# Experts and last sums of a two-block transformer in the block of the routing, without the two joins of all engines

## Reference, cut to what matters

```python
def hier_moe(h, w_group, b_group, w_expert, b_expert, w_gate_e, w_up_e, w_down_e):
...
    weight = p_grp[:, None] * jax.nn.softmax(top_v, axis=-1)
    eid = (grp[:, None] * EXPERTS_PER_GROUP + top_i).reshape(-1)
...
    def expert_block(args):
        xb, e = args
        return (jax.nn.silu(xb @ w_gate_e[e]) * (xb @ w_up_e[e])) @ w_down_e[e]
...
    y_slot = yb[dest] * w_f[order][:, None].astype(yb.dtype)
    y = jnp.zeros((N, D), h.dtype).at[tok[order]].add(y_slot)

# second_block, end
        x = x + hier_moe(rms_norm_2(x, norm_ffn_g[l]), ...)
    return rms_norm_2(x, norm_final_g)
```

## Time and profile before

| | |
|---|---|
| time, median of 3 runs | 3125.62 us (3123.28 to 3128.7) |
| profiled execution, its own time | 3124.2 us |
| its span, first to last instruction | 3122.4 us |
| mean granted TensorE clock | 0.978 |
| PE busy | 2990.5 us, 96% of the span |
| DVE, ACT, POOL busy | 1374.4, 903.4, 267.6 us |

### The profile page before, as it was taken

How to read it: one execution, slowest core, us unless ns; L and a number is a source line. 1 busy time by engine, 2 the same in 40 slices (tenths; PEclk the granted TensorE clock), 3 DMA queues, 4 the chain that set the end, 5 groups by cost and what they waited for, 6 DMA issues and landing times. The chain is left out here.

```text
span 3122.4 us, 38269 instructions
## 1 busy us (share of the span) xinstructions
PE 2990.5 (96%) x15170; PEld 2323.6 (74%) x15170; DVE 1374.4 (44%) x2200; ACT 903.4 (29%) x1423; POOL 267.6 (9%) x310
## 2 busy tenths in 40 slices
PE   9999999999999999999999999999999988989995
PEld 7888888877746788888888887888888865864442
DVE  5636343445586564654333334333332267521113
ACT  4111111232265322223212233222233255321111
POOL 1000000001100100001000011000010155012221
PEclk9999999999999999999999999999999989989997
DMA  7232323221000464543232212223232200438995
GB/s 281 99 119 102 126 100 124 89 69 55 28 1 28 146 236 177 217 160 101 88 113 90 86 41 81 94 94 108 77 115 94 101 28 1 180 128 359 370 364 201
DMA packets 78207, 395.81 MB, mean 127 GB/s; under 512 B 17536, under 2 KB 19968, under 8 KB 51328
## 3 DMA queue, kind: packets, MB, share of 16 engines
q1 hardware_dynamic: 66560, 385.65, 33.7%
q0 software_dynamic: 11520, 8.43, 0.9%
HBM read 444.34 MB, written 16.78 MB: 148 GB/s over the span
## 5 line engine op out<-in xcount | busy, mean ns | idle before, releaser
L849 PE MATMUL ps<-h_high_ffn,weights_high_ffn 128*128 128x512 f32 (+1 forms) x1696 | 623.1, 367 | 4.0 <-DVE weights_low_ffn L991 4.0
L850 PE MATMUL ps<-h_low_ffn,weights_high_ffn 128*128 128x512 f32 (+1 forms) x1696 | 622.9, 367 | 0.0
L851 PE MATMUL ps<-h_high_ffn,weights_low_ffn 128*128 128x512 f32 (+1 forms) x1696 | 622.5, 367 | 0.0
L849 PEld LDWEIGHTS ps<-h_high_ffn,weights_high_ffn 128*128 128x128 f32 x1696 | 319.8, 189 | 57.7 <-issue 5.1
L850 PEld LDWEIGHTS ps<-h_low_ffn,weights_high_ffn 128*128 128x128 f32 x1696 | 319.9, 189 | 52.7
L851 PEld LDWEIGHTS ps<-h_high_ffn,weights_low_ffn 128*128 128x128 f32 x1696 | 319.7, 188 | 52.9
L938 ACT ACTIVATE weights_high_ffn<-weights 128x2048 fp32r<-128x2048 f32 (+4 forms) x160 | 243.7, 1523 | 343.2 <-PE ps L851 276.6
L849 PE MATMUL ps<-hidden_high_ffn,weights_high_ffn 128*128 128x512 f32 (+1 forms) x880 | 327.2, 372 | 14.0 <-issue 6.9
L850 PE MATMUL ps<-hidden_low_ffn,weights_high_ffn 128*128 128x512 f32 (+1 forms) x880 | 325.8, 370 | 0.0
L991 DVE TENSOR_TENSOR weights_low_ffn<-weights,weights_high_ffn 128x2048 fp32r<-128x2048 f32 (+4 forms) x160 | 289.6, 1810 | 81.2 <-ACT weights_high_ffn L938 79.7
L851 PE MATMUL ps<-hidden_high_ffn,weights_low_ffn 128*128 128x512 f32 (+1 forms) x880 | 325.2, 370 | 0.0
(11 more groups left out here) (459 smaller groups left out, 4502.8 us busy)
## 6 DMA issues: line engine op xcount, KB each, us to landing
weights<-in_ffn_gu SPq DMA_DIRECT2D x88, 1024.0 KB, 4.9
big<-in_w_exp_gu SPq DMA_DIRECT2D x32, 2048.0 KB, 10.0
scratch_ffn<-in_w_mod SPq DMA_DIRECT2D x35, 1536.0 KB, 6.5
weights<-in_ffn_d SPq DMA_DIRECT2D x24, 768.0 KB, 4.3
weights<-in_w_in SPq DMA_DIRECT2D x16, 1024.0 KB, 4.8
weights<-in_ffn_d SPq DMA_DIRECT2D x24, 640.0 KB, 3.9
weights<-in_w_exp_dn SPq DMA_DIRECT2D x15, 1024.0 KB
hbuf<-in_w_exp_dn SPq DMA_DIRECT2D x12, 1024.0 KB
```

Source lines behind the costliest of these rows:

```text
L849: pe.matmul(out, wh, xh, start=(k == 0), stop=False)
L850: pe.matmul(out, wh, xl, start=False, stop=False)
L851: mm = pe.matmul(out, wl, xh, start=False, stop=(k == n - 1))
```

## The change

`experts` and `combine` no longer open a block of their own; their lists are appended to those of the block that already holds branches, merge and routing. Both joins go, with their drains and branches. Where they ordered something that no semaphore did, waits are written: PE waits, after the 30 matmuls and ahead of the first `turn`, for the last copy of turned rows on ACT and for the last step of the routing on DVE (`routed`). SP waits for 23 of 24 gate and up products before it loads the gain, which now goes to `work[:, 7 * D:8 * D]` in place of `work[:, 0:D]`.

```diff
-    def experts():
+    def experts(block):
...
+        routed = dve_chain.at
...
-        with nc.Block() as block:
+        if True:
             @block.sync
             def _(sync):
                 for n in range(2, NP):
...
                 keep_busy(pe, 30, 7)
+                pe.wait_ge(turn_ev[0].sem, turn_ev[0].at)
+                pe.wait_ge(dve_chain.sem, routed)
                 in_order(turn, gate_up, hidden_turn, down)
...
-    def combine():
+    def combine(block):
...
-        gain = work[:, 0:D]
+        gain = work[:, 7 * D:8 * D]
...
-        with nc.Block() as block:
+        if True:
             @block.sync
             def _(sync):
+                sync.wait_ge(hidden_mm.sem, PAIRS - 1)
                 sync.dma_start(gain, io["final_gain"]).then_inc(tables.sem, 16)
...
         merge_and_route(block, G, O_high, O_low, U_high, U_low, w_high, w_low)
-    experts()
-    combine()
+        experts(block)
+        combine(block)
```

## The result

The changed kernel took 3103.85 us (median of 6 runs, 3097.23 to 3109.36) beside 3122.78 us of the kernel before in the same comparison; the ratio is 0.9934, 95% interval 0.9921 to 0.9946. The ratio stands for 20.6 us less where 17.8 were forecast (0.9943, inside the interval); the two medians are 18.9 apart. It is faster, as forecast; whether the 2.8 us between 20.6 and 17.8 belong to the change is the question that the experiments had to answer.

What follows compares the result with a forecast made beforehand. PE, busy 96% of the span, was taken to bound the kernel. Terms of 10.2, 6.2 and 1.4 us sum to 17.8, taken off the earlier median 3125.62 to give 3107.8 us; range 3103 to 3114.5.

Steps and rivals of the forecast that it cites:

- First join removed: Boundary from routing to experts: PE goes straight into the 30 matmuls, first turn at 2776.9 instead of 2787.10, 10.2 us.
- Experts shifted and not stretched: Experts stage: weight loads move forward with PE, so the 10.2 us arrive at its end whole.
- Second join removed: Boundary from experts to last sums: SP waits for the scatters only, first load of pair_rows 6.2 us earlier.
- Gain moved: Start of the last sums: gain loaded early, so DVE starts 1.4 us sooner after the first load, then works 15.96 us.
- The sum: Whole kernel: 10.2 + 6.2 + 1.4 = 17.8 us less.
- The level and the range: Whole kernel: 3107.8 us, from the earlier median 3125.62 less 17.8, with a range of 3103 to 3114.5.
- A: Whole kernel, likeliest case: all terms as worked out, 3107.8 us, within some 3103 to 3112; chance 0.80.
- D: First boundary: gather 0 comes late, PE stands after the 30 matmuls and starts at half clock; 3119.7 us, chance 0.04.
- E: Experts: PE's clock falls after the 30 matmuls and stays down through many pairs; slower, 3131.8 us, chance 0.02.
- B: Second boundary: the scatter's completion takes POOL's drain, so 6.2 us stay; 3114.0 us, chance 0.09.
- C: Experts stage: bound by its transfers, the earlier start turns into waits on weights; 7.6 us left, 3118.0 us, chance 0.04.

Runs made afterwards that it cites:

- identity_12: The changed kernel with 12 identity matmuls in place of 30 ahead of the experts; ratio 0.9958 to the kernel before.
- identity_0: The changed kernel without any identity matmul ahead of the experts; ratio 0.995 to the kernel before.
- again: The changed kernel measured once more with no edit; median 3104.71 us, ratio 0.9939 to the kernel before; its profiled execution took 3118.38 us.
- second_join_only: The kernel before with only the second join removed and the gain loaded early; 3117.2 us, ratio 0.9983 to the kernel before.
- gather_alone: The changed kernel with 12 identity matmuls, gather 1 issued only when gather 0 has landed; single execution, first turn 7.95 us after L2852 starts.

## Why the prediction was right or wrong

**First join removed: right, a little small.** 10.2 was forecast, 10.7 it is. The term summed durations from the rows, 1.99 + 7.10, while records on PE overlap: the first identity pass starts 1.82 us after L2852 and the turn 6.77 after that.

**Experts shifted and not stretched: right**, 300.33 us in the changed kernel and 300.01 with only the first join removed, 300.24 before.

**Second join removed: right in its mechanism**, 6.2 forecast and 5.9 found: the load follows the scatter's start by 2.13 us and not by 1.9.

**Gain moved: mis-sized.** DVE's start came 1.4 us sooner after the issue, as forecast. "Behind it DVE works for 15.96 us as before; the later tiles are 0.5 MB ahead too" is what failed in this term. DVE begins 1.4 us sooner, the tiles of the second 128 tokens do not come as much sooner, and its work takes 16.6 to 17.4 us in the three traces of the changed kernel. With the 0.4 us of issue that the gain's place also costs, and which my sum had in its second term, the move is worth about 0.9 and not 1.8.

**The sum: right, with some luck.** The first term's missing 0.5 and the gain's 1.0 too much partly cancel. 17.8 forecast, 16.9 in the rows of the first pair of traces, 17.3 from the two joins apart, 18.2 to 18.8 with 2.6 to either side from all runs.

**The level and the range: wrong, and this is the step that failed.** "3125.62 - 17.8" set the forecast on the median of three runs of before; the six of the comparison have 3122.78, and 41 runs 3123.28. The same 17.8 us taken off 3122.78 is 3105.0, and all 18 runs of the changed kernel have the median 3105.05; a range as wide as mine around 3105.0 would have begun at 3100.2 and held the 3102.2. Its lower end was A's spread, "from the bounds of its terms ... and from the 5.4 us between the runs of before". Nor was 5.4 us the spread: the runs of the changed kernel lie between 3096.8 and 3118.4, those of before between 3118.0 and 3141.1. The row that would have warned me was in the page of the profile: a mean clock of 0.978 in a program whose PE is busy for 96%. I looked at the clock only where the change was, and named the half clock (D, E) only as something the change could cause. I did not ask how much of the time before it hung on the clock.

**B, C, D, E: not seen**, B and C refuted by rows (the load in the middle of the drain; the experts' 300.0 us), D and E not entered: gather 0 was in before the 30 matmuls ended. What D feared is what `identity_12` and `identity_0` show, at 1.9 and 3.0 us. E priced a microsecond at half clock at half a microsecond; in the branches it cost about 0.35.

Shown: both boundary terms and their adding up, in rows; the wait that takes back most of the gain's earlier start; the clock's part in the stage ahead, by its traces and by the filled gaps. Open: the gain's worth to better than half a us; what makes up the 8 us of scatter outside that stage; what decides in one execution whether this stage has 10 or 55 us at half clock in the same code; and what POOL's drain waits for: it lasts 7.6 us beside an empty transfer and ends 5.7 us behind the last packet, so it is not the transfer's data.

## What to carry to other kernels

Each join of all engines here cost what the slowest drain cost, and that was POOL's behind its indirect DMAs (6.4 and 7.6 us), not the data's arrival; waits on the landings alone gave 16.6 us. Matmuls that keep the clock up are sized by what they cover: with the join gone the 30 still had to span a gather of 4.4 us, and with fewer the clock's fall cost more than the earlier start gave. Before a difference of half a per cent is explained or a range is set, lay the unchanged stages of the two traces side by side and look at their clock.

## What the hardware did that I had not expected

- TensorE at 0.50 for 41 us on end in one execution (the four windows of `again` above are of it) and for 3.4 to 20.5 us in the other ten with the same code, in a stage that begins with gaps of about 1 us in PE and shows busy shares of 0.88 and more at half clock; one us at half clock in this stage cost about a third of a us (16.0 us longer with 44.4 us more of it).
- The clock fell when PE had stood 2.5 us in the kernel before, 2.9 in `identity_12` (2767.3 to 2770.2), 3.0 in `identity_0` and 3.2 in `second_join_only`. In `gather_alone` it was still 1.00 through a gap of 3.2 us and fell at 2773.0, 0.4 us after PE had gone on.
- A gather of half of 0.69 MB was seen by PE 4.4 to 4.7 us after its issue, an empty scatter by SP after 2.1. The section of the Trainium skill's page "DMA: Bandwidth & Descriptors" named above would put the gather at 2.8 us (an estimate: 2.0 plus 0.35 MB at 436 GB/s); the traces have 1.6 to 1.9 us more.
- A POOL drain of 6.3 to 7.8 us behind indirect DMAs. It ended 0.4 us after the last packet at the first boundary and 5.7 us after it at the second.
